# Last query projection of the attention layer cut into five parts inside the head-pair loop

## The reference, cut to what matters

```
qg = h @ w_qg                                   # 16 query heads of 64, and gates
q = qg[..., :1024].reshape(b, t, 4, 4, 64) * 64 ** -0.5
k_c, v_c = compress_blocks(...)                 # 15 compressed keys and values per group
p_c = masked_softmax(q . k_c);   o_c = p_c @ v_c
p_s = masked_softmax(q . k_slc); o_s = p_s @ v_slc   # all blocks are chosen at 256 tokens
p_w = masked_softmax(q . k_win); o_w = p_w @ v_win
o = g0 * o_c + g1 * o_s + g2 * o_w
return o @ w_o
```

## Time and profile before

| | us |
|---|---|
| median of 3 runs (968.77 to 970.65) | 969.88 |
| the profiled execution's own time | 969.67 |
| its span, first to last instruction | 967.9 |
| granted TensorE clock, mean over the span | 0.997 of full speed |
| TensorE busy | 926.8 |
| VectorE busy | 583.4 |
| ScalarE busy | 520.0 |

### The profile page before, as it was taken

How to read it: one execution, slowest core, us unless ns; L and a number is a source line. 1 busy time by engine, 2 the same in 40 slices (tenths; PEclk the granted TensorE clock), 3 DMA queues, 4 the chain that set the end, 5 groups by cost and what they waited for, 6 DMA issues and landing times.

```text
span 967.9 us, 14303 instructions
## 1 busy us (share of the span) xinstructions
PE 926.8 (96%) x5437; PEld 781.8 (81%) x5437; DVE 583.4 (60%) x967; ACT 520.0 (54%) x920; POOL 24.2 (2%) x47
## 2 busy tenths in 40 slices
PE   6999999999999999999999999998889999999998
PEld 6988978797888877888878788997567788888776
DVE  5767875666566564555544665656857555554465
ACT  6644545766767456444434548245865644444352
POOL 5100000000000000000000000000000000000000
PEclk9999999999999999999999999999999999999999
DMA  9941202021112556767545654420024566555552
GB/s 318 333 138 44 88 0 88 12 77 44 45 45 92 206 163 212 239 219 249 197 161 186 205 174 159 147 88 2 1 88 143 168 193 191 175 191 176 170 187 101
DMA packets 105899, 138.30 MB, mean 143 GB/s; under 512 B 4585, under 2 KB 76786, under 8 KB 105842
## 3 DMA queue, kind: packets, MB, share of 16 engines
q1 hardware_dynamic: 103650, 130.15, 42.1%
q0 software_dynamic: 2160, 7.36, 2.2%
q10 hardware_dynamic: 32, 0.01, 0.0%
HBM read 136.45 MB, written 1.05 MB: 142 GB/s over the span
## 4 chain that ended last, share of the span: by engine, by line
PE 79%; ACT 10%; DVE 8%; issue 2%; DMA 0%; ACTq 0%; SPq 0%; DVEq 0%
PE ps L497 16%; PE ps L499 16%; PE ps L498 16%; PE ps L476 4%; PE ps L481 4%; ACT w_hi L1105 4%; PE ps L483 4%; PE ps L482 4%; DVE w_lo L1565 4%; PE ps L712 3%; PE ps L730 3%; PE ps L945 1%; PE ps L991 1%; ACT qkvT L1499 1%; PE ps L615 1%
## 5 line engine op out<-in xcount | busy, mean ns | idle before, releaser
L1565 DVE TENSOR_TENSOR w_lo<-w_raw,w_hi 128x2048 fp32r<-128x2048 f32 (+2 forms) x100 | 220.7, 2207 | 210.3 <-ACT w_hi L1105 210.1
L1105 ACT ACTIVATE w_hi<-w_raw 128x2048 fp32r<-128x2048 f32 (+2 forms) x100 | 184.4, 1844 | 191.6 <-PE ps L499 149.4
L497 PE MATMUL ps<-w_hi,x_hi 128*128 128x512 f32 x480 | 193.1, 402 | 7.3 <-DVE gdn L1776 2.2
L499 PE MATMUL ps<-w_hi,x_lo 128*128 128x512 f32 x480 | 187.6, 391 | 0.0
L498 PE MATMUL ps<-w_lo,x_hi 128*128 128x512 f32 x480 | 187.3, 390 | 0.0
L497 PEld LDWEIGHTS ps<-w_hi,x_hi 128*128 128x128 f32 x480 | 90.2, 188 | 29.8 <-issue 7.4
L499 PEld LDWEIGHTS ps<-w_hi,x_lo 128*128 128x128 f32 x480 | 90.1, 188 | 19.4
L498 PEld LDWEIGHTS ps<-w_lo,x_hi 128*128 128x128 f32 x480 | 90.3, 188 | 16.7
L481 PE MATMUL ps<-x_hi,w_hi 128*128 128x256 f32 x320 | 91.9, 287 | 0.3 <-DVE w_lo L1611 0.3
L497 PE MATMUL ps<-w_hi,big 128*128 128x512 f32 x224 | 89.9, 401 | 1.0 <-DVE w_lo L1565 1.0
L482 PE MATMUL ps<-x_lo,w_hi 128*128 128x256 f32 x320 | 90.7, 283 | 0.0
(11 more groups left out here) (309 smaller groups left out, 1513.9 us busy)
## 6 DMA issues: line engine op xcount, KB each, us to landing
w_raw<-in_ffn_w_in SPq DMA_DIRECT2D x88, 512.0 KB, 4.6
w_raw<-in_ffn_w_out SPq DMA_DIRECT2D x40, 512.0 KB, 4.0
w_raw<-in_gdn_w_in SPq DMA_DIRECT2D x28, 512.0 KB, 4.7
gdn<-in_gdn_w_in SPq DMA_DIRECT2D x20, 512.0 KB, 8.7
w_raw<-in_gdn_w_out SPq DMA_DIRECT2D x16, 512.0 KB, 4.5
w_raw<-in_ple_w_gate SPq DMA_DIRECT2D x16, 512.0 KB, 4.6
w_raw<-in_kv_w SPq DMA_DIRECT2D x12, 512.0 KB, 4.2
qkvT<-in_cmp_w POOLq DMA_DIRECT2D x8, 512.0 KB, 5.5
```

Source lines behind the costliest of these rows:

```text
L497: mm(o, hi, w_h, start=first and kk == 0, stop=False, skip_group_check=True)
L499: return mm(o, lo, w_h, start=False, stop=end and kk == n - 1, skip_group_check=True)
L1105: A(whi[:, place(stage, q), c0:c0 + n], ring_raw(u) if stage == "qkv" else raw[:, q, 0:n], ACT.Copy).then_inc(S["hi_done"], 1)
L1565: V.tensor_tensor(wlo[:, s, c0:c0 + n], ring_raw(u) if stage == "qkv" else raw[:, q, 0:n], whi[:, s, c0:c0 + n], ALU.subtract).then_inc(S[ ...
```

## The change

The last query unit is issued as 16 items of three matmuls: four after scores(2, 0) in turn 1, then three ahead of and three behind output(1), and three ahead of and three behind output(2). It accumulates in bank 1 all that time, so the outputs of pairs 0 to 4 all go to bank 0 (`out_bank`), and output(p) for these waits for out_lo(p-1) in place of out_lo(p-2). q_out(3) moves from ahead of the loop into turn 3 on VectorE. The second half of the compressed branch moves by two turns: cmp_scores(1) and cmp_shifted(1) from turn 1 to turn 3, cmp_exp(1) from after exps(2) to after exps(4), cmp_weighted(1) from turn 2 to turn 4, and cmp_turned(1) with cmp_copy(1) from the end of turn 3 to the middle of turn 5, ahead of turned(5, 0). output(4) and out_hi(4) go behind turned(5, 1). No instruction is added or taken away.

```diff
@@ -272,6 +272,9 @@
             j, n = divmod(head, 4)
             return 2 * j + n if n < 2 else HK + 2 * j + n - 2
 
+        def out_bank(p):
+            return 0 if p < 5 else p % 2
+
         def ring_raw(u):
 
             s = u % RING
@@ -1005,7 +1008,7 @@
                         pe.wait_ge(S["pts_act"], 4 * p + 2 * e + b - 1)
                     if p == 0 and b == 0:
                         pe.wait_ge(S["cs_dve"], 1)
-                    if p == 4 and b:
+                    if p == 5 and b:
                         pe.wait_ge(S["pct_sb"], 2)
                     o = bank(6 + b, 3, P)
                     transpose(o[:, 0, :], pr0[:, p % 2, e, b, :])
@@ -1020,11 +1023,13 @@
                 if p == 0:
                     pe.wait_ge(S["pct_sb"], 1)
                     pe.wait_ge(S["fx_dve"], NG)
-                if p == 1:
+                if p == 4:
+                    pe.wait_ge(S["pct_sb"], 2)
+                if p == 5:
                     pe.wait_ge(S["cs_dve"], 10)
-                if p >= 2:
-                    pe.wait_ge(S["alo"], p - 1)
-                o = [ps[halves[e], par, 0:T] for e in range(2)]
+                if p:
+                    pe.wait_ge(S["alo"], p if p < 5 else p - 1)
+                o = [ps[halves[e], out_bank(p), 0:T] for e in range(2)]
                 for b in range(2):
                     vb = [vtk[:, s, b, ND * g:ND * g + ND] for s in range(2)]
                     for e in range(2):
@@ -1049,27 +1054,48 @@
             scores(1, 1)
             turned(0, 0)
             turned(0, 1)
-            stage_unit("q", 1, x_hi, x_lo, 1, 1)
             pe.wait_ge(S["q_sb"], 3)
             cmp_turned(0, 0)
+
+            def last_queries(items):
+
+                if items[0] == 0:
+                    pe.wait_ge(S["lo_done"], U0["q"] + 4)
+                for n in items:
+                    tile, k = divmod(n, KD)
+                    last = unit_products(place("q", 1), 1, x_hi, x_lo, tile, k, k == 0, k == KD - 1)
+                if items[-1] == 2 * KD - 1:
+                    last.then_inc(S["unit_done"], 1)
+
             for p in range(1, 8):
-                if p > 1:
+                if p == 2:
+                    last_queries(range(4, 7))
+                if p == 3:
+                    last_queries(range(10, 13))
+                if p > 1 and p != 5:
                     output(p - 1)
+                if p == 2:
+                    last_queries(range(7, 10))
+                if p == 3:
+                    last_queries(range(13, 16))
                 if p < 7:
-                    if p == 1:
-                        pe.wait_ge(S["q_sb"], 3)
+                    if p == 5:
+                        pe.wait_ge(S["q_sb"], 4)
                     scores(p + 1, 0)
+                if p == 1:
+                    last_queries(range(0, 4))
+                if p == 5:
+                    pe.wait_ge(S["pts_act"], 20)
+                    cmp_turned(1, 7)
                 turned(p, 0)
                 if p < 7:
                     scores(p + 1, 1)
                 turned(p, 1)
-                if p == 1:
+                if p == 3:
                     pe.wait_ge(S["q_sb"], 4)
                     cmp_scores(1, 1)
-                    output(0)
-                if p == 3:
-                    pe.wait_ge(S["pts_act"], 16)
-                    cmp_turned(1, 7)
+                if p in (1, 5):
+                    output(p - 1)
             pe.wait_ge(S["p_act"], 16)
             post_stage("wo", (4, 4), ((4, 5), (2, 3)), big_tok8, lambda k: pe.wait_ge(S["alo"], k + 1),
                        lambda u: output(7) if u == 0 else None)
@@ -1515,7 +1541,7 @@
             def out_hi(p):
 
                 act.wait_ge(S["av_ps"], p + 1)
-                A(big[:, p, :], bank(p % 2, T), ACT.Copy).then_inc(S["ahi"], 1)
+                A(big[:, p, :], bank(out_bank(p), T), ACT.Copy).then_inc(S["ahi"], 1)
 
             def wo_quarter(m):
                 u, part = divmod(m, 4)
@@ -1532,19 +1558,19 @@
             exps(1)
             cmp_copy(0, 0)
             for p in range(1, 8):
-                if p > 1:
+                if p > 1 and p != 5:
                     out_hi(p - 1)
+                if p == 5:
+                    cmp_copy(1, 7)
                 turned(p, 0)
                 for m in ((0,), (1,), (2,), (3,), (4,), (5,), (6, 7))[p - 1]:
                     wo_quarter(m)
                 turned(p, 1)
-                if p == 1:
-                    out_hi(0)
-                if p == 3:
-                    cmp_copy(1, 7)
+                if p in (1, 5):
+                    out_hi(p - 1)
                 if p < 7:
                     exps(p + 1)
-                if p == 1:
+                if p == 3:
                     cmp_exp(1)
             out_hi(7)
             post(2, "wo", ((4, 5), (2, 3)), "fin1")
@@ -2115,7 +2141,7 @@
             def out_lo(p):
 
                 dve.wait_ge(S["ahi"], p + 1)
-                V.tensor_tensor(big[:, KD + p, :], bank(p % 2, T), big[:, p, :], ALU.subtract).then_inc(S["alo"], 1)
+                V.tensor_tensor(big[:, KD + p, :], bank(out_bank(p), T), big[:, p, :], ALU.subtract).then_inc(S["alo"], 1)
 
             split("q", 0, 1)
             q_out(0)
@@ -2157,19 +2183,20 @@
                 for e in range(2):
                     maxima(1, e, t)
             cmp_weighted(0)
-            q_out(3)
             for p in range(1, 8):
                 weights(p, 0)
                 if p < 7:
                     maxima(p + 1, 0, 0)
                     maxima(p + 1, 1, 0)
+                if p == 3:
+                    q_out(3)
                 weights(p, 1)
                 if p < 7:
                     maxima(p + 1, 0, 1)
                     maxima(p + 1, 1, 1)
-                if p == 1:
+                if p == 3:
                     cmp_shifted(1, 1)
-                if p == 2:
+                if p == 4:
                     cmp_weighted(1)
                 out_lo(p - 1)
                 if p >= 3:
```

## The result

| | before | after |
|---|---|---|
| median of 6 runs, us | 969.41 (968.74 to 970.65) | 979.34 (978.27 to 979.69) |
| ratio, 95% interval | | 1.010 (1.0087 to 1.0113) |
| span of the profiled execution | 967.9 | 977.6 |
| mean granted TensorE clock | 0.997 | 0.990 |

The change makes the kernel 9.9 us slower. The forecast was +3.0 us, 972.9 us, with a range to 975.8, so the direction was right and the size was far off, outside the range. The profile's page of the changed kernel: its first row, TensorE's busy tenths and the granted clock, each digit one fortieth of the span.

The account below looks back on a forecast made before the run. The prediction took TensorE, busy 96% of the span, as the bound, with the loop a ring of waits. Its terms -2.2 + 0.1 + 0.9 + 1.6 + 0 + 2.6 gave +3.0 us, 972.9, range 970.8 to 975.8.

Parts of the forecast that it names:

- 1, lead: From cmp_scores(0) to turn 1: the query unit leaves its place, so turn 1 starts earlier; -2.2 us.
- 2, turn 1: Turn 1: cmp_scores(1) leaves, ten items arrive, and TensorE's own work sets the length, 10.97 against 10.83; +0.1 us.
- 3, turn 2: Turn 2: six items, 2.2 us of matmuls, enter a wait of 1.05; +0.9 us.
- 4, turn 3: Turn 3: q_out(3) partly shows and output(3) waits for out_lo(2) behind cmp_shifted(1); +1.6 us.
- 5, turn 4: Turn 4: output(4) leaves but the length stays about 6.8 us; 0, bounds 0 to +0.5 us.
- 6, turn 5: Turn 5: cmp_turned(1) with cmp_copy(1) delays turned(5, 0), and out_hi(4) waits for output(4); +2.6 us.
- rival A: TensorE's clock falls in the new 3.6 us wait ahead of cmp_turned(0), adding 2.9: +5.9 us, 975.8; chance 8%.
- the ring: Loop cycle of scores, transposes, copies and exponentials, each waiting on another engine; said to set turns of about 6.8 us.
- B: Turn 3: the wait for the shared bank is hidden, so no measurable change, +0.9 us, 970.8; chance 17%.
- C: Turns 1 to 3: the moved parts fill TensorE's waits, so faster, -3.5 us, 966.4; chance 6%.

Follow-up runs that it names:

- a2_fill_all: Changed kernel with unread filler matmuls in three TensorE waits: 27 ahead of cmp_turned(0), 16 ahead of output(3), 19 ahead of scores(6, 0); +5.1 us against before.
- a1_fill1: Changed kernel with 27 unread filler matmuls in the wait ahead of cmp_turned(0); +8.0 us against before.
- c2_shifted: Changed kernel with out_lo(2) ahead of cmp_shifted(1) and 12 filler matmuls ahead of cmp_scores(0); +9.1 us against before.
- b4_reordered: Changed kernel reordered: ten query items ahead of cmp_turned(0), compressed half's pieces and out_lo(1) moved, output(4) and out_hi(4) back; 966.59 us, -3.0 against before.
- a4_unit_whole: Changed kernel with the query unit back in one piece ahead of cmp_turned(0); +6.9 us against before.
- b1_items_first: Changed kernel with ten query items ahead of cmp_turned(0), three ahead of and three behind output(1); +4.1 us against before.
- c1_fill2: Changed kernel with 16 unread filler matmuls only in the wait ahead of output(3); +8.3 us against before.
- a3_outlo_first: Changed kernel with out_lo(2) on VectorE ahead of cmp_shifted(1) in turn 3; +5.7 us against before.
- b3_before_gap_fill: Kernel before, with the whole last query unit moved behind scores(2, 0) and 27 filler matmuls in the resulting wait; +3.1 us against before.
- c3_both: Changed kernel with ten items ahead of cmp_turned(0), three each side of output(1), and out_lo(2) ahead of cmp_shifted(1); +1.9 us against before.

## Why the prediction was wrong, step by step

The order's terms, read at full clock in a2_fill_all against before, and the clock in the change against a2_fill_all:

| step | forecast | measured |
|---|---|---|
| 1, lead | -2.2 | -2.13 |
| 2, turn 1 | +0.1 | +0.69 |
| 3, turn 2 | +0.9 | +1.15 |
| 4, turn 3 | +1.6 | +1.86 |
| 5, turn 4 | 0 | +0.16 |
| 6, turn 5 | +2.6 | +2.71 |
| clock | 0 (rival A: +2.9) | +5.67 |
| sum | +3.0 | +10.11 |

Steps 1 and 4 to 6 held, with the waits where they were said to be: the start of output(3) came 4.01 us after that of cmp_scores(1) in a1_fill1, where the sum had 3.93. Step 1 took 0.07 us for a semaphore, which no row showed; the changed trace has 0.14, from the end of cmp_weighted(0) at 662.79 to 662.93. Steps 2 and 3 were sized too low: I took 0.122 us a matmul from a whole unit, but a piece of nine takes 1.27 us to the next start, not 1.10, and an output with a piece behind it 1.88, not 1.78. Five pieces and the changed neighbours make 0.8 us over the two turns.

The step that failed is the clock, which the sum put at nothing: it cost 5.67 us, more than the whole order. The forecast held the clock full, and rival A let it fall once, behind the 3.6 us of step 1, at 8%. It gave against it that the granted clock was 1.00 in the loop before. That was no evidence, since the longest single wait of TensorE there was 1.1 us:

```profile
PE ps L991 <- ACT qkvT L1499: 3.2, 5, 1.1
```

And the trace of before does hold a fall, outside the loop, which the forecast did not use. In the first layer TensorE, after steady work, waits 1.64 us, and the granted clock falls about 1.2 us after that wait has ended (columns of the second view as in the earlier trace rows):

```profile
121.72 2.77 PE L662 MATMUL ps<-tri_gt,gdn 128*128 128x128 f32 x16 [1.64 <-DVE gdn L1701]
```

```profile
120.00:122.00 2.00, 0.36 (x3) 0.28 (x3) 2.00 (x5) 1.42 (x6) 0.00 (x0) 1.00 0.00 0
122.00:124.00 2.00, 2.00 (x15) 2.00 (x15) 2.00 (x6) 0.60 (x1) 0.00 (x0) 0.72 0.00 0
124.00:126.00 2.00, 2.00 (x12) 1.94 (x11) 1.30 (x4) 0.60 (x1) 0.00 (x0) 0.50 0.00 0
```

So a wait less than half as long as the one of step 1 was followed by a fall in the very trace that the forecast was read from. All 14 traces have this wait, and 9 of them this fall. With it cmp_scores(0) starts at 652.08 to 653.63 us (c2_shifted, with its added matmuls, left out), without it at 650.73 to 652.56. What rival A did rest on, is weaker: the matmuls there are 0.22 us apart, but the granted clock of that stretch reads 1.00 in the profile.

The sum itself predicted one wait of over 3 us and one of 2.1, and turn 4 without output(4) leaves a third of 3.1, which I did not write down since it cost nothing in the ring. Only the first was put to the question of the clock. The price of that one was about right, 2.15 us in lead and turn 1 (0.42 + 1.73) against rival A's 2.9, since the work took less than twice as long (scores(2, 0) 1.59 us to the next start in place of 0.87) and the clock was back just before the four items were through. What rival A lacked was the two others: 2.39 in turns 3 and 4 (1.72 + 0.67) and 1.14 in turn 5.

The Trainium skill, "TensorE: Matmul & The Clock Gate", The HAM clock gate, bears on it more than I allowed: a fall of the clock behind idle stretches is what its section describes. The trace agrees on the fall, 0.50 behind all three waits. It does not agree on the size of the gap: the section warns of gaps longer than the 2.14 us of output(3), and the measurement decides.

Rivals B and C: the shared bank's wait was not hidden, and the items did not fit the waits they were put in. That the idea of C can work in another order is shown by b4_reordered. The chances don't add up as said: a tenth less of the forecast's 69%, with A's 8%, gives 0.70 for slower, not 0.75, and leaves 0.24 for within.

## What to carry to other kernels

On a kernel bound by TensorE, work moved out of a place must be matched by what TensorE will wait for there; a wait that was covered by 5.8 us of matmuls became 3.5 us of idling, and the low clock behind it cost 2.15 us more. List every new wait of TensorE, also those that cost nothing in the order. Then look through the whole trace that you have, not only the part that you change, for the longest waits of TensorE and the granted clock in the microseconds behind them. Price each new wait by that, or by an experiment. Put the filler where a dependent chain on another engine ends late, keep the release of a shared bank ahead of a long chain, and keep copies that free nothing urgent off the ring.

## What the runs showed of the hardware

The 14 traces, one execution of each kernel, show this of the granted clock behind a wait of TensorE (the first 20 us of the span, where it reads 1.00 throughout, are left out):

| wait, us | fell to 0.50 | where |
|---|---|---|
| 1.2 to 1.5 | 0 of 44 | outside the loop, all traces |
| 1.64 | 9 of 14 | first layer, at about 122 us |
| 2.08 to 2.14 | 5 of 5 | output(3) in the change, a1_fill1, a4_unit_whole, b1_items_first; a later projection in c1_fill2 |
| 3.09 to 3.10 | 8 of 9 | ahead of scores(6, 0); not in a3_outlo_first |
| 3.46 | 5 of 5 | ahead of cmp_turned(0) |

In the loop it also stayed 1.00 behind the waits of 0.99 to 1.1 us. Why the same wait is followed by a fall in one kernel's trace and not in another's is open. The fall came inside the wait or up to about 1.4 us after its end. Filling a wait with matmuls whose result nobody reads kept the clock up each time (six waits in a1_fill1, a2_fill_all, b3_before_gap_fill and c1_fill2). The low stretch also differed in length between like kernels: turn 3 was 10.94 in b1_items_first and 11.70 in a4_unit_whole. The executions of one kernel differ too: those of c3_both that took 969.3 and 969.5 us had mean clocks of 0.998 and 1.000, the other eight, 970.6 to 972.4 us, 0.994 to 0.998. The kernel before itself ranged from 968.2 to 970.9 us on one chip. So differences of 1 us between timed medians of four executions are not to be read.
